# Fourteen filler products on TensorE at every norm of a two-block transformer kernel

## What is computed

```python
def rmsnorm(x, g):
    xf = x.astype(jnp.float32)
    y = xf * lax.rsqrt(jnp.mean(xf * xf, axis=-1, keepdims=True) + RMS_EPS)
    return (y * g.astype(jnp.float32)).astype(x.dtype)
...
        h = rmsnorm(x, ffn_norm[i])
        g, u = jnp.split(h @ ffn_w_in[i], 2, axis=-1)
        x = x + (jax.nn.silu(g) * u) @ ffn_w_down[i]
```

## Time and profile before

| | us |
|---|---|
| median of three runs | 3904.36 |
| the three runs | 3902.45, 3904.36, 3916.76 |
| span of the profiled execution | 3913.5 |
| PE busy in it | 3561.7 (91%) |
| DVE busy | 1622.9 (41%) |
| ACT busy | 1410.3 (36%) |
| POOL busy | 1529.0 (39%) |

### The profile page before, as it was taken

How to read it: one execution, slowest core, us unless ns; L and a number is a source line. 1 busy time by engine, 2 the same in 40 slices (tenths; PEclk the granted TensorE clock), 3 DMA queues, 4 the chain that set the end, 5 groups by cost and what they waited for, 6 DMA issues and landing times.

```text
span 3913.5 us, 47994 instructions
## 1 busy us (share of the span) xinstructions
PE 3561.7 (91%) x17554; PEld 2882.4 (74%) x17554; DVE 1622.9 (41%) x2641; ACT 1410.3 (36%) x2658; POOL 1529.0 (39%) x1376
## 2 busy tenths in 40 slices
PE   6898999899999997999899977888888889999998
PEld 4677888777777886788788866777777777457886
DVE  4873331225743321432246665555566540114321
ACT  3363332224643332433234433333333332013332
POOL 4235445442444455444522213233323233034444
PEclk8999999898999998999989988898898999999999
DMA  3102333320012332233321110111111113232332
GB/s 115 54 17 68 96 97 95 85 82 1 1 44 81 96 97 81 81 96 92 86 55 49 44 33 23 32 33 33 33 28 33 28 33 81 75 89 83 96 92 75
DMA packets 471305, 245.79 MB, mean 63 GB/s; under 512 B 13819, under 2 KB 468710, under 8 KB 471014
## 3 DMA queue, kind: packets, MB, share of 16 engines
q1 hardware_dynamic: 468464, 239.10, 21.4%
q10 hardware_dynamic: 2678, 4.53, 0.4%
HBM read 241.51 MB, written 2.10 MB: 62 GB/s over the span
## 4 chain that ended last, share of the span: by engine, by line
PE 80%; DVE 10%; ACT 4%; issue 3%; POOL 1%; ACTq 0%; DMA 0%; DVEq 0%; POOLq 0%
PE ps L428 16%; PE ps L429 16%; PE ps L430 16%; PE ps L452 4%; PE ps L1253 3%; PE ps L1233 2%; PE ps L1883 2%; PE ps L1868 2%; PE ps L1799 2%; PE ps L1887 2%; PE ps L1800 2%; PE ps L1801 2%; PE ps L1242 1%; PE ps L1435 1%; PE ps L445 1%
## 5 line engine op out<-in xcount | busy, mean ns | idle before, releaser
L412 POOL TENSOR_TENSOR w_lo<-ring,w_hi 128x512 fp32r<-128x512 f32 (+1 forms) x860 | 1123.8, 1328 | 1797.3 <-ACT w_hi L403 1797.3
L403 ACT ACTIVATE w_hi<-ring 128x512 fp32r<-128x512 f32 (+1 forms) x860 | 488.5, 617 | 1479.6 <-PE ps L430 1272.4
L428 PE MATMUL ps<-h_hi,w_hi 128*128 128x512 f32 x2136 | 857.2, 401 | 59.3 <-POOL h_lo L585 35.1
L430 PE MATMUL ps<-h_hi,w_lo 128*128 128x512 f32 x2136 | 842.4, 394 | 0.0
L429 PE MATMUL ps<-h_lo,w_hi 128*128 128x512 f32 x1744 | 685.1, 393 | 0.0
L428 PEld LDWEIGHTS ps<-h_hi,w_hi 128*128 128x128 f32 x2136 | 409.0, 191 | 162.8 <-issue 60.1
L430 PEld LDWEIGHTS ps<-h_hi,w_lo 128*128 128x128 f32 x2136 | 407.7, 191 | 87.1
L429 PEld LDWEIGHTS ps<-h_lo,w_hi 128*128 128x128 f32 x1744 | 331.5, 190 | 71.1 <-issue 3.4
L682 DVE TENSOR_TENSOR silu_g<-ps,silu_g 128x512 f32<-128x512 f32 x88 | 60.9, 692 | 612.1 <-PE ps L430 612.1
L429 PE MATMUL ps<-a_lo,w_hi 128*128 128x512 f32 x768 | 300.1, 391 | 0.0
L430 PE MATMUL ps<-a_hi,w_lo 128*128 128x512 f32 x704 | 274.2, 390 | 0.0
(11 more groups left out here) (366 smaller groups left out, 6158.2 us busy)
## 6 DMA issues: line engine op xcount, KB each, us to landing
ring<-in_ffn_w_in SPq DMA_DIRECT2D x176, 512.0 KB, 3.8
ring<-in_w_in SPq DMA_DIRECT2D x96, 512.0 KB, 4.0
ring<-in_ffn_w_down SPq DMA_DIRECT2D x32, 512.0 KB, 3.6
ring<-in_ffn_w_out SPq DMA_DIRECT2D x32, 512.0 KB, 3.7
ring<-in_w_o SPq DMA_DIRECT2D x16, 512.0 KB, 3.7
ring<-in_w_branch_gdn SPq DMA_DIRECT2D x16, 512.0 KB, 3.6
ring<-in_nsa_w_in SPq DMA_DIRECT2D x15, 512.0 KB, 3.7
ring<-in_dsa_w_in SPq DMA_DIRECT2D x13, 512.0 KB, 4.0
```

Source lines behind the costliest of these rows:

```text
L403: act.activation(w_hi[:, (halves(u) + j) % PIECES, 0:n, :], slot(u)[:, j * n:(j + 1) * n, :], ACT.Copy) \
L412: pool.tensor_tensor(w_lo[:, q % PIECES, 0:n, :], slot(u)[:, j * n:(j + 1) * n, :], w_hi[:, q % PIECES, 0:n, :].bitcast(f32), ALU.subtract ...
L428: pe.matmul(dst, wh, hi(k), start=first and k == 0, stop=False)
L430: ins = pe.matmul(dst, wl, hi(k), start=False, stop=last and k == 2 * n - 1)
```

## The change

After the sum of squares is complete, and after its semaphore has been raised, `pe_norm` issues fourteen more f32 products: the ones matrix as weights, 256 columns of constants (the identity and the ones) as the moving operand, into bank 6. Each starts and ends its own sum, and nothing reads the result. They wait for nothing and raise no semaphore. `pe_norm` is called at all nine norms, outside any loop.

```diff
         pe.matmul(ps[:, 7, :], ones, squares[:, (KT - 1) % 2, :], start=False, stop=True) \
           .then_inc(sig("norm_sum").sem, 1)
+        ident_and_ones = cst[:, const_cols["ident"][0]:const_cols["ones"][1]]
+        for _ in range(FILLERS):
+            pe.matmul(ps[:, 6, 0:2 * P], ones, ident_and_ones, start=True, stop=True)
+
+    FILLERS = 14
```

## The result

The changed kernel takes 3920.69 us (median of 20 runs, 3910.28 to 3927.18), the kernel before 3916.14 us (median of 20 runs beside it, 3898.22 to 3919.38). The ratio is 1.0022, 95% interval 1.0011 to 1.0032: some 8.6 us slower, small, but clear of zero. The forecast was 3909.1 us, 4.7 above the median then known, and called it the same.

A forecast was written before the change was run, and what follows sets the result against it. PE's own time was taken to set most of the span, with slow products at norms hidden behind tile waits. Layer 0's +4.7 and eight zeros on the median 3904.36 gave 3909.1 us, range 3896 to 3923.

The forecast's parts named there:

- The slow products are hidden behind the tiles: First units after norms: PE waits 0.83 us for POOL's tile 6 even at half clock, so faster products gain 0.
- rival 2: All slow products at five norms, gates unit and `final` were on the path: -19.7 us, 3884.7; chance 0.04.
- Price of a pass, 0.213 us: Each norm's 28 filler passes: 0.213 us apiece at full clock, 5.97 us in all; 11.95 at half.
- the cover at the FFN norms, `mix_norm`, `mid`, `ffn1_norm`: Fillers fit in PE's idle time after the sum, 1.6 us to spare at FFN norms, 10.4 at `mid`: 0 us.
- The gates unit stays at half clock: Behind layer 1's attention norm: 6.5 us idle remains after the fillers, clock falls again; 0 us, bound -8.
- `final`: Last norm: fillers leave 3.9 us idle before the transposes, just above the longest fall time; 0 us, -1 kept as bound.
- Layer 0's start, +4.7: Attention norm of layer 0: fillers delay the memory's transposes, ACT's copies and the first unit's tile 6 by 4.7 us.
- the bounds of the prediction: Layer 0's start: +4.0 us if the clock rises at once, +5.2 at the slowest rise.
- Either answer costs and gives nothing: First units after FFN norms: whether or not the clock holds through the last 1.6 us idle, 0 us.
- the zeros of the sum: The eight norms other than layer 0's attention norm: each put at 0 us.
- The base: Starting time for the forecast: median of three runs, 3904.36 us, not the profiled execution's 3913.5.
- About 0.5%: Whole kernel: smallest difference a measurement can tell from no change, 19.5 us, so the forecast was called the same.

The follow-up runs named there:

- e6: 36 fillers at the FFN norms of both layers, `mix_norm` and `ffn2_norm`, none elsewhere, against the kernel before: ratio 1.0042, 16 us slower.
- e4: Fillers sized to reach the next product, 27 at layer 1's attention norm, 37 at `mid`, 22 at `final`, against the kernel before: ratio 0.9985, 5.9 us faster.
- e7: As e4, plus fillers between tiles and after token groups in the gates unit, against the kernel before: ratio 0.9980.
- e1: 14 fillers at the attention norm of layer 0 alone, against the kernel before: ratio 1.0016, 6.2 us slower.
- e11: The changed kernel plus five fillers in the mixer's gap, against the kernel before: ratio 0.9992, median 3911.16 us.
- e12: Five fillers in the mixer's gap and 14 at layer 0's attention norm alone, against the kernel before: ratio 0.9994; 0.0017 (6.6 us) above e9.
- e2: 14 fillers at all norms but the attention norm of layer 0, against the kernel before: ratio 1.0011, 4.3 us slower.
- e13: Five fillers in the mixer's gap and 14 at the eight norms other than layer 0's attention, against the kernel before: ratio 0.9985; 0.0008 (3.1 us) above e9.
- e9: No fillers at norms, five in the mixer's gap ahead of the first head's last level, against the kernel before: ratio 0.9977, median 3903.66 us.
- e5: 27 fillers at the FFN norms of both layers, `mix_norm` and `ffn2_norm`, none elsewhere, against the kernel before: ratio 0.9992.

## Why the prediction was right and where it was wrong

- **The slow products are hidden behind the tiles: right.** Tile 6 did not move at the norms, and e6 met the slack to 0.2 us. But that a faster PE makes the wait for tile 6 longer (rival 2) was wrong: it stayed at 0.84 us, and PE waited ahead of tiles 3 and 4 instead.
- **Price of a pass, 0.213 us; the cover at the FFN norms, `mix_norm`, `mid`, `ffn1_norm`: right.** 28 passes took 6.21 us with the last one's own end; at `ffn1_norm` 0.30 us of cover remained, 0.5 was forecast.
- **The gates unit stays at half clock: right**, and e4 and e7 showed that even a full clock at its start is lost inside it.
- **`final`: right.** The transposes still ran at half clock after 3.55 us of idle time.
- **Layer 0's start, +4.7: right in kind.** The profile shows 3.9 at the copies and 3.5 at tile 6 of the change's own. The fillers ended at 36.2, 0.3 earlier than worked out, for the clock rose at 30.0 and not at 31.24. Where it rose later, at 32.2 in e1 and 32.5 in e11, tile 6 came 25.2 and 25.0 us after the start of L556's passes instead of 20.1 before and 23.7 in the changed kernel: 3.5 to 5 us, about the bounds of the prediction. By ratios e1 and e12 put it at 6.2 and 6.6, uncertain by 4 and 5 us.
- **"Either answer costs and gives nothing" at the first units: wrong, and so are the zeros of the sum that rest on it.** I asked whether the clock would hold through the 1.6 us ahead of the unit, and not what it would do inside the unit. Before, slow products filled PE up to tile 6 and brought the clock up by then. Fast ones leave gaps between the tiles, and a fall that comes then costs 0.2 to 2.2 us after tile 6, where nothing hides it. Some executions have it, some do not: 2.8 us in each of the profiles of e2, e11 and e13, nothing in that of the change. By ratios it is 4.3 us in e2 (0.4 to 8.6) and 3.1 in e13 over e9, where zero lies within the uncertainty.
- **The base: wrong.** I put the change's 4.7 us on the median of three runs, 3904.36, two of which were of the kernel's lower group, while the profiled execution was of the upper one. Its time is its span plus 1.8 us, so 3913.5 is 3915.3, close to the median of twenty, 3916.14. The same sum on it gives 3920.0, against 3920.69 measured; that they meet so closely is partly luck, for the sum has 4.7 us at the start, where 3.5 were seen, and none of what other stretches added. I had seen the 9.1 us between span and median and called it scatter.
- **"About 0.5%" as what a measurement can tell from no change: wrong.** Twenty runs of each told it to 0.1% (1.0011 to 1.0032), so the 4.7 us of the sum, 0.12%, are just within reach and no reason to expect the same.
- **The groups' shares: no term for them.** The kernel before was in its lower group in 29 of 121 runs; in the changed kernel, e1 and e2 it is 2 of 44 (3910.28, far below the changed kernel's others, and 3907.53 of e1). In the measured comparison itself the kernel before had 6 runs in the lower group (mean 3902.1) and 14 in the upper (mean 3916.9). The changed kernel's mean, 3920.6, is 3.8 us above that of the 14, and the 6 account for the other 4.4 of the 8.2 us between the means. So about half of what was measured is the group of the mixer's unit, and the rest is in reach of what the norms' fillers cost, 3.8 us here and 6.6 in e11 against e9, uncertain by 2.0 and 1.5 us. Why the share should fall was not shown, and six runs of twenty can be chance in part; e4, e5 and e7, with 5, 6 and 9 of 12 runs in the lower group, show only that it differs between kernels.

## What to carry to other kernels

Before an engine is kept warm for the next stage, look for the wait that ends last inside that stage: here a tile made by other engines came after even the slow products were done, so their speed was worth nothing, and making them fast opened gaps in which the clock could fall. Filler work belongs only where the engine is idle by the trace and the next work on it sets the time and keeps the clock that it begins with: the mixer's unit did and gained 10 us, the gates unit did not and gained nothing. In front of work that another engine waits for (the transposes at the start) it is paid in full. And when a few runs lie further apart than their own noise, find out which group the profile is from before a forecast is put on their median.

## What the runs showed of the hardware that was not expected

- A clock that is full when a stage begins can fall within it: after 6 us with PE busy for 3.69 of them (e2), and in a unit of thin products that keep PE busy without a gap (e7, at 748.8, after 4 us with PE busy for all of them).
- A unit of thin products can stay at half clock though PE is never idle. The gates unit of 36-column products stayed at 0.50 for over 20 us, and at 1.00 it did not stay (e4, e7). The mixer's 96 products of 128 columns ran at 0.50 or at 1.00 from end to end (20 us or 10.6), by what the clock did at their start.
- That one change of the clock was 10 of the some 11 us between the two groups of the kernel before. Five f32 products of 256 columns ahead of it, 2.3 us of work in idle time, removed it.
